# Who subtracts the low halves of the weights: VectorE call by call, or GpSimd in one stream

## The reference

```
h = rmsnorm(x, g);  proj = h @ w_in            # and so on, some 19 weight matrices
x = x + rmsnorm(f, g_post_ffn)                  # end of the first block
a, b = split(rmsnorm_2(x, norm_ffn) @ w_ffn_in) # feed-forward of the second block
x = x + (silu(a) * b) @ w_ffn_out
```

## Time and profile before

| | us |
|---|---|
| median of 3 runs | 1704.19 (1703.19 to 1706.45) |
| profiled execution, first to last instruction (span) | 1701.9 |
| TensorE matmul busy | 1630.8 (96%) |
| VectorE busy | 925.6 (54%) |
| ScalarE busy | 620.5 (36%) |
| GpSimd busy | 26.1 (2%) |

### The profile page before, as it was taken

One profiled execution on the slowest core, in us unless ns is written; L12 is line 12 of the kernel. 1 busy time (PEld: TensorE's weight loads), 2 busy tenths in 40 slices (PEclk: granted clock), 3 DMA queues, 4 the chain that ended last, 5 costly groups with the idle time before them and its releaser, 6 DMA issues.

```text
span 1701.9 us, 20773 instructions
## 1 busy us (share of the span) xinstructions
PE 1630.8 (96%) x7854; PEld 1342.2 (79%) x7854; DVE 925.6 (54%) x1471; ACT 620.5 (36%) x856; POOL 26.1 (2%) x17
## 2 busy tenths in 40 slices
PE   5999999999998999999999899899899999999999
PEld 5788666888876788888888668899668788888887
DVE  6343365644544777777334768888844444444322
ACT  6241333432233444444233355454334232222211
POOL 0000000000000000000001000110000000000000
PEclk9999999999998999999999999999558999999999
DMA  6402221222222122223323212022001222222332
GB/s 232 142 26 100 71 72 50 96 79 96 99 99 99 48 100 99 99 99 113 109 99 113 75 53 97 25 75 75 1 1 50 92 106 99 94 89 92 113 107 74
DMA packets 24890, 147.11 MB, mean 86 GB/s; under 512 B 2515, under 2 KB 5075, under 8 KB 8316
## 3 DMA queue, kind: packets, MB, share of 16 engines
q1 hardware_dynamic: 24828, 146.27, 24.7%
HBM read 144.13 MB, written 2.13 MB: 86 GB/s over the span
## 4 chain that ended last, share of the span: by engine, by line
PE 89%; DVE 5%; ACT 3%; issue 2%; DMA 0%; DVEq 0%; SPq 0%; ACTq 0%
PE bank L1537 26%; PE bank L1539 25%; PE bank L1538 25%; PE bank L1631 4%; PE bank L1649 3%; PE bank L1638 2%; PE bank L1881 1%; ACT w_hi L544 1%; PE bank L1851 1%; DVE w_lo L947 1%; PE bank L1660 1%; PE bank L1590 0%; DMA vec<-vec 0%; DVE diag L1001 0%; DVE h_lo L1016 0%
## 5 line engine op out<-in xcount | busy, mean ns | idle before, releaser
L947 DVE TENSOR_TENSOR w_lo<-raw,w_hi 128x2048 fp32r<-128x2048 f32 x123 | 281.8, 2291 | 400.6 <-ACT w_hi L544 400.3
L1537 PE MATMUL bank<-h_hi,w_hi 128*128 128x512 f32 (+1 forms) x1200 | 476.0, 397 | 11.1 <-DVE h_lo L1016 9.9
L1539 PE MATMUL bank<-h_hi,w_lo 128*128 128x512 f32 (+1 forms) x1200 | 470.1, 392 | 0.0
L1538 PE MATMUL bank<-h_lo,w_hi 128*128 128x512 f32 (+1 forms) x1200 | 469.7, 391 | 0.0
L544 ACT ACTIVATE w_hi<-raw 128x2048 fp32r<-128x2048 f32 x129 | 246.3, 1910 | 353.7 <-PE bank L1539 352.0
L1537 PEld LDWEIGHTS bank<-h_hi,w_hi 128*128 128x128 f32 (+1 forms) x1200 | 226.2, 188 | 65.1 <-DVE h_lo L1016 9.8
L1539 PEld LDWEIGHTS bank<-h_hi,w_lo 128*128 128x128 f32 (+1 forms) x1200 | 226.0, 188 | 49.1
L1538 PEld LDWEIGHTS bank<-h_lo,w_hi 128*128 128x128 f32 (+1 forms) x1200 | 226.3, 189 | 47.3 <-issue 1.0
L1537 PE MATMUL bank<-a_hi,w_hi 128*128 128x512 f32 x352 | 136.9, 389 | 0.0
L1538 PE MATMUL bank<-a_lo,w_hi 128*128 128x512 f32 x352 | 136.9, 389 | 0.0
L1539 PE MATMUL bank<-a_hi,w_lo 128*128 128x512 f32 x352 | 136.9, 389 | 0.0
(11 more groups left out here) (247 smaller groups left out, 2048.2 us busy)
## 6 DMA issues: line engine op xcount, KB each, us to landing
raw<-weights SPq DMA_DIRECT2D x129, 1024.0 KB, 4.8
toep<-bias_scratch SPq DMA_DIRECT2D x8, 448.0 KB, 4.6
x<-xT SPq DMA_DIRECT2D x1, 2048.0 KB, 14.7
outT<-x SPq DMA_DIRECT2D x8, 256.0 KB, 4.3
memT<-memT SPq DMA_DIRECT2D x1, 1024.0 KB, 5.9
mem2T<-mem2T SPq DMA_DIRECT2D x1, 1024.0 KB, 5.5
masks_in<-masks SPq DMA_DIRECT2D x1, 512.0 KB, 3.3
vec<-vec SPq DMA_DIRECT2D x1, 140.0 KB, 5.7
```

The costliest lines, as they stand in the source:

```text
L947: nc.vector.tensor_tensor(w_lo[m % 2][:, :], raw[m % 2][:, :], w_hi[m % 2][:, :].bitcast(F32), ALU.subtract).then_inc(lo_ready, 1)
L1537: nc.tensor.matmul(o, lh, rh, start=first, stop=False)
L1538: nc.tensor.matmul(o, lh, rl, start=False, stop=False)
L1539: return nc.tensor.matmul(o, ll, rh, start=False, stop=last)
```

## The change

VectorE's helpers `split_w` and `split_part` are gone, with all their calls. GpSimd gets a helper of the same name that makes the low halves of a range of slices, whole, one after the other, in the order of the loads. Before each it waits for its own one before (`lo_ready`) and for the rounding (`hi_ready`). Its earlier work stands between ranges: the masks and the fill of `sel` and `sfx`, which came right after the start, now follow the slices `mem_kv_2`, `idx` and the first of `hf`, and at every level from the second on one slice follows the suffix addition. The other engines' programs are as they were.

```diff
@@ gpsimd
             nc.gpsimd.memset(relb[NB:NB + 1, :], NEG).then_inc(set_up, 1)
+
+            def split_w(first, last):
+
+                for m in range(first, last):
+                    if m > first:
+                        pool.wait_ge(lo_ready, m)
+                    pool.wait_ge(hi_ready, m + 1)
+                    nc.gpsimd.tensor_tensor(w_lo[m % 2][:, :], raw[m % 2][:, :], w_hi[m % 2][:, :].bitcast(F32),
+                                            ALU.subtract).then_inc(lo_ready, 1)
+
+            pool.wait_ge(set_up, 2)
+            split_w(0, FIRST["iq"])
+            pool.wait_ge(lo_ready, FIRST["iq"])
             pool.wait_ge(mask_in, 32)
             nc.gpsimd.tensor_copy(masks[:, :, :], masks_in[:, :, :]).then_inc(set_up, 1)
             pool.wait_ge(set_up, 3)
+            split_w(FIRST["iq"], FIRST["idx"] + 1)
+            pool.wait_ge(lo_ready, FIRST["idx"] + 1)
             nc.gpsimd.memset(sel[:, :, :], 0.0).then_inc(set_up, 1)
             pool.wait_ge(set_up, 4)
+            split_w(FIRST["hf"], FIRST["hf"] + 1)
+            pool.wait_ge(lo_ready, FIRST["hf"] + 1)
             nc.gpsimd.memset(sfx[:, :], 0.0).then_inc(set_up, 1)
...
             nc.gpsimd.memset(aT[:, :, :], 0.0).then_inc(set_up, 1)
+            pool.wait_ge(set_up, 6)
+            split_w(FIRST["hf"] + 1, FIRST["sq"] + 2)
+            pool.wait_ge(lo_ready, FIRST["sq"] + 2)
...
                                         ALU.add).then_inc(suffix_ready, 1)
+                if lv:
+                    pool.wait_ge(suffix_ready, lv + 1)
+                    split_w(FIRST["sq"] + lv + 1, FIRST["sq"] + lv + 2)
+                    pool.wait_ge(lo_ready, FIRST["sq"] + lv + 2)
+            split_w(FIRST["sq"] + LEVELS + 1, NLOADS)
@@ vector
-            def split_w(m, i=None, per=0):
-
-                if i is None and m >= NLOADS:
-                    return
-                dve.wait_ge(hi_ready, m + 1 if i is None else m + 1 + per * i)
-                nc.vector.tensor_tensor(w_lo[m % 2][:, :], raw[m % 2][:, :], w_hi[m % 2][:, :].bitcast(F32),
-                                        ALU.subtract).then_inc(lo_ready, 1)
...
                 for m in range(loads):
-                    split_w(FIRST[name] + m + 1)
                     for t in (2 * m, 2 * m + 1):
...
             residual("mix", lambda j: mixed[:, j, :], "g_post_mix", "g_pre_ffn", range(KT))
-            split_w(FIRST["up"] + 2)
             norm_scale("ffn", S)
...
                 for m in range(2):
-                    if i is not None:
-                        split_w(FIRST["up"] + m + 4, i, 2)
-                    elif m:
-                        split_w(FIRST["up"] + 3)
                     for c in (2 * m, 2 * m + 1):
```

More of the change, by code:

```diff
@@ L1102, in _ @@
                 add_squares(j == 0, M, ssq_mem)
-                if j == 1:
-                    split_w(0)
-            split_w(1)
             dve.wait_ge(const_in, 32)
@@ L1109, in _ @@
                 add_squares(j == 0)
-                if j == 2:
-                    split_w(2)
                 if j == 5:
                     norm_scale("mem", M, keep=8)
-                    split_w(3)
                     dve.wait_ge(bank_free[6], turn(("spread", "mem")) + 1)
@@ L1119, in _ @@
                                                                     ALU.mult))
-            split_w(4)
-            split_w(5)
-            split_w(6)
             norm_scale("x", S, keep=0)
@@ L1127, in _ @@
                 normal("qm", t, qm[:, t, :])
-            split_w(FIRST["v"] + 1)
-            attention("mem", MHEADS * TT, None, lambda h, i: o_tok[:, i, h * MDH:(h + 1) * MDH],
-                      between=lambda s: s in (8, 9) and split_part(FIRST["q"], s - 8))
+            attention("mem", MHEADS * TT, None, lambda h, i: o_tok[:, i, h * MDH:(h + 1) * MDH])
             turned("turn_mem", 4, lambda j: br_hi[:, 8 + j, :], lambda j: br_lo[:, 8 + j, :])
@@ L1133, in _ @@
             times_rms("k", 2, lambda t: k[:, t, :])
-            split_w(FIRST["cc"] + 1)
             def toeplitz(h, i):
@@ L1141, in conv_branch @@
             def conv_branch(s):
-                for part_ in range(2):
-                    if s - part_ in CONV_STEPS:
-                        split_part(FIRST["cc"] + 2 + CONV_STEPS.index(s - part_), part_)
                 if s - 1 in CONV_TILE[4:8]:
@@ L1182, in _ @@
                     for m in range(3):
-                        split_w(FIRST["branch"] + 3 * half + m + 1, i, 6)
                         for t in range(2 * m, 2 * m + 2) if m < 2 else ():
@@ L1202, in _ @@
             for m in range(4):
-                split_w(FIRST["w_out"] + m + 1)
                 for j in (2 * m, 2 * m + 1):
@@ L1206, in _ @@
             norm_scale("mix", S)
-            split_w(FIRST["up"] + 1)
             wait_free(("w_out", KT - 1))
             residual("mix", lambda j: mixed[:, j, :], "g_post_mix", "g_pre_ffn", range(KT))
-            split_w(FIRST["up"] + 2)
             norm_scale("ffn", S)
@@ L1257, in _ @@
                 for m in range(3):
-                    if 3 * g + m + 2 <= 12:
-                        split_w(FIRST["down"] + 3 * g + m + 2)
                     if m:
@@ L1266, in _ @@
             norm_scale("down", S, extra=M)
-            split_w(FIRST["mem_kv_2"] + 1)
             dve.wait_ge(bank_free[3], turn(("down", 3), 1) + 1)
[L1270 to L1274, removed]
             out_tile = lambda j: down[:, j * S:(j + 1) * S]
-            residual("down", out_tile, "g_post_ffn", "norm_mix_2", range(4), between)
+            residual("down", out_tile, "g_post_ffn", "norm_mix_2", range(4))
             dve.wait_ge(w_used, FIRST["mem_kv_2"] + 2)
             residual("down", out_tile, "g_post_ffn", "norm_mix_2", range(4, KT))
-            split_w(FIRST["idx"])
             norm_scale("x_2", S, keep=0)
@@ L1309, in _ @@
                                          vec[:, VEC["sa_q_gain"]:VEC["sa_q_gain"] + 2], 64 ** -0.5, None, ALU.mult))
-            split_w(FIRST["hf"])
             dve.wait_ge(set_up, 4)
@@ L1340, in _ @@
             for m in range(2):
-                if m == 0:
-                    split_w(FIRST["hf"] + 1)
                 for t in (2 * m, 2 * m + 1):
@@ L1345, in _ @@
                     normal("hf", t, lf[:, t * S:(t + 1) * S])
-                split_w(FIRST["hf"] + m + 2)
                 top_keys(5 * m, 5 * m + 5)
@@ L1356, in _ @@
                     normal("hq", t, qf[:, t * S:(t + 1) * S])
-                split_w(FIRST["hq"] + m + 2)
                 top_keys(10 + 5 * m, 15 + 5 * m)
@@ L1383, in _ @@
                 if lv == LEVELS:
-                    split_w(FIRST["sq"] + lv + 1)
                     break
@@ L1402, in _ @@
                     head_norm(tok, tok_sq, S)
-                if lv:
-                    split_w(FIRST["sq"] + lv + 1)
                 top_keys((20, 24, 24, 24, 28, 28, 31)[lv], (24, 24, 24, 28, 28, 31, 34)[lv])
@@ L1466, in _ @@
             for m in range(4):
-                split_w(FIRST["w_out_2"] + m + 1)
                 for j in (2 * m, 2 * m + 1):
@@ L1474, in _ @@
                     add_squares(j == 0)
-            split_w(FIRST["up_2"] + 1)
-            split_w(FIRST["up_2"] + 2)
             norm_scale("ffn_2", S)
@@ L1482, in up_2_turn @@
                 it = 0 if i is None else i + 1
-                if i is not None:
-                    split_w(FIRST["up_2"] + 4, i, 2)
                 dve.wait_ge(prod, FT + 2 * it)
@@ L1488, in up_2_turn @@
                     normal(name, c, y[c][:, :])
[L1489 to L1492, removed]
                 dve.wait_ge(a_down, FT + 2 + 2 * it)
@@ L1510, in _ @@
             for g in range(4):
-                for m in range(3):
-                    split_w(FIRST["down_2"] + 3 * g + m + 2)
                 for j in (2 * g, 2 * g + 1):
```

## The result

| us | before | after |
|---|---|---|
| median of 4 runs each | 1704.84 (1703.19 to 1706.45) | 1744.86 (1743.46 to 1745.81) |
| ratio, 95% interval | | 1.0236 [1.0224, 1.0248] |
| span of the profiled execution | 1701.9 | 1743.3 |

The change makes the kernel 2.4% slower. Forecast were 1752 us within 1718 to 1788. On the span +47.5 was forecast and +41.4 came.

The account below looks back on a forecast made before the run. TensorE was taken to hold 89% of the path, VectorE 5%. Place terms of 42.5 us plus 5 for the clock, 47.5, on the 1701.9 span gave 1749.4; the median, 2.3 above the span, gave 1752 us (1718 to 1788).

Parts of the forecast that it names:

- Duration, 4.5 us: One GpSimd subtraction of 2048 elements takes 4.5 us (4.1 to 6.7), twice the corrected mean suffix addition.
- Start, +9: First four slices: 4.5 us locks delay VectorE's low halves and sums, and the scaling by 9.1 us; +9 us.
- Attention with convolution, +1, and memory attention, 0: Attention with convolution: VectorE relieved of six subtractions, then locked, +1 us (-1 to +4); no term for memory attention.
- `br_lo`, +4.5: GpSimd's subtraction takes the port pair amid eight two-input subtractions that TensorE consumes one by one; +4.5 us (0 to 4.5).
- Loop over `up`, 1.5 + 3: Subtraction stalls TensorE +1.5 us; turns of 22.0 us, 0.25 above TensorE, over 10 turns, plus 0.4 at entry: +3.
- Levels and last scaling, 1.1 + 4.2 + 3.3 + 2.1 = 10.7: Subtractions behind suffix additions lock VectorE: level 1 +1.1, level 2 +4.2, level 4 +3.3, last scaling +2.1 us.
- Norm of `ffn_2` and second slice of `up_2`, 1.5 + 2.2 = 3.7: Norm's products wait for GpSimd's subtraction, +1.5 us; at the second slice TensorE already waited for the subtraction, +2.2 us.
- Clock, +5: TensorE runs at a lower clock after new stands of 4 us or more; +5 us (0 to 12).
- half the locks: Rival: locks bite half as often, as waiting VectorE instructions may get in between subtractions; about 1731 us, chance 0.22.
- slow GpSimd: Rival: a GpSimd subtraction takes 5.5 us, the loop over `up` turns in 23.9 us; about 1788 us, chance 0.12.
- faster: Rival: GpSimd's subtraction holds nobody, what counts is 281.8 us off VectorE; about -4 us, 1700 us, chance 0.05.
- even: Rival: losses fall into unseen slack, so the time stays within 0.2%; chance 0.05.

Follow-up runs that it names:

- Experiment 1: Kernel before, with GpSimd making 11 of the 129 low halves (slices 8, 14 to 18, 80 to 84): 1700.09 us against 1704.38, ratio 0.9975.
- experiment 2: Kernel before, with GpSimd making 74 low halves (slices 8 to 36, 64 to 73, 80 to 84, 99 to 128): 1697.87 us, ratio 0.9959.
- experiment 7: Changed kernel, with the start's slices 0 to 7 subtracted by VectorE as before: 1736.03 us.
- experiment 8: Changed kernel, with slices 44 to 63, the loop over `up`, subtracted by VectorE again: 1739.45 us.
- experiment 4: Changed kernel, with the levels' seven slices 85 to 91 subtracted by VectorE as before: 1728.62 us.
- experiment 5: Changed kernel, all 129 low halves on GpSimd, which waits for VectorE's work at seven places (`br_lo` and levels): 1722.69 us.
- experiment 6: Changed kernel, with each GpSimd subtraction cut into four instructions of 512 elements, the signal on the last: 1735.14 us.

## Why the prediction was right, and where its terms were off

The rule was right as the prediction put it: the two engines exclude each other for a whole instruction, and the price is paid by VectorE operations of two SBUF inputs and SBUF scalar ones. The place-by-place sum is less good than its total, which came close by offsetting misses. In the trace after, the rows at level 2 that answer to the earlier trace rows show each link. The subtraction starts behind the suffix addition, 1.0 us before z ends (the prediction had it wait for z's end). It takes 5.48 us, because z still runs. `lf`, 1.23 us before, takes 5.29 and ends 1.08 us behind the subtraction:

```profile
1116.42 2.96 POOL L537 TENSOR_TENSOR sfx<-sfx,lf 128x1024 f32<-128x1024 f32 x1 [17.01 <-ACT ex L875]
1117.06 3.40 DVE L1358 TENSOR_TENSOR z<-qf,ex 128x1024 f32<-128x1024 f32 x1
1119.45 5.48 POOL L505 TENSOR_TENSOR w_lo<-raw,w_hi 128x2048 fp32r<-128x2048 f32 x1
1120.72 5.29 DVE L1364 TENSOR_TENSOR lf<-lf 128x1024 f32<-128x1024 f32 x1 [0.26 <-DVE z L1358]
...
1130.22 1.97 PE L1613 MATMUL bank<-ident,tok 128*128 128x128 f32 x8 [5.07 <-DVE tok L1267]
```

Step by step, on the span:

- *Duration, 4.5 us:* the rows are 4.50 at least and mostly 4.58 to 4.62, mean 4.64 with waits. The sum of seven suffix additions less three waits was good to 0.1. The Trainium skill's figure (GPSIMD Engine Reference, 3.1: 4497 ns) is the shortest row.
- *Start, +9:* +7.2. The replay held: the second rounding came 2.1 us late (2.2 forecast), the second subtraction ended 4.5 late (4.5), the third 6.8 late (6.4). The scaling behind the fourth subtraction came 8.3 us late (43.67 against 35.36), not 9.1, and TensorE's next wait, for `mk`, was 1.69 us in place of 2.59.
- *Attention with convolution, +1, and memory attention, 0:* -2.6 and -2.0. This is the largest miss, 5.6 us. I looked for what the lock adds, saw slack, and did not ask who waited for VectorE's subtraction there. The kernel before has TensorE waits of 1.35 us at 102.67 and 0.63 at 278.66 in just these stretches, behind `row` and its maximum, which read PSUM. Experiment 1 shows that this gain is real and can be had by itself. Of the 4.6 us gained, 2.4 are stands and 2.2 matmul time, mostly at a higher granted clock.
- *`br_lo`, +4.5:* +6.1. 0.7 of it is the last gate, which experiment 2 shows and which the prediction had at nothing. TensorE stands 3.57 us in the middle of the eight low parts (rows below) and then runs at the lower clock for a while; the stretch from rounding 37 to 38 cost 5.5, 3.9 and 3.9 us in three executions with the same order (the changed kernel and experiments 7 and 8). The stand is the term, the rest is the clock: between these roundings it was granted 0.90 in the changed kernel and 1.00 in the two others.

```profile
500.10 9.24 DVE L1014 TENSOR_TENSOR br_lo<-merged,br_hi 128x512 fp32r<-128x512 f32 x8
502.80 4.79 POOL L505 TENSOR_TENSOR w_lo<-raw,w_hi 128x2048 fp32r<-128x2048 f32 x1 [7.71 <-ACT w_hi L569]
508.19 0.50 PE L1490 MATMUL bank<-br_hi,w_hi 128*128 128x512 f32 x1 [3.57 <-DVE br_lo L1014]
```

- *Norms of `mix` and `ffn`, 1.4 and 1.5:* 1.1 and 1.65.
- *Loop over `up`, 1.5 + 3:* 4.3, of which 1.9 are the two stands at the entry and 2.4 the longer turns. The turn is 21.98 us where 22.0 was forecast, with twice a convolution step that starts inside GpSimd's subtraction and ends 0.54 us behind it. The rows answer to the earlier trace rows:

```profile
620.43 1.90 ACT L569 ACTIVATE w_hi<-raw 128x2048 fp32r<-128x2048 f32 x1
622.48 4.61 POOL L505 TENSOR_TENSOR w_lo<-raw,w_hi 128x2048 fp32r<-128x2048 f32 x1 [5.63 <-ACT w_hi L569]
623.18 4.45 DVE L1215 SCALAR_TENSOR_TENSOR y<-tap,vec,y 128x511 f32<-128x511 f32 x1 [2.00 <-ACT y L765]
...
634.22 4.61 POOL L505 TENSOR_TENSOR w_lo<-raw,w_hi 128x2048 fp32r<-128x2048 f32 x1 [7.13 <-ACT w_hi L569]
634.97 4.41 DVE L1215 SCALAR_TENSOR_TENSOR y<-tap,vec,y 128x511 f32<-128x511 f32 x1 [0.64 <-ACT y L765]
...
642.41 1.90 ACT L569 ACTIVATE w_hi<-raw 128x2048 fp32r<-128x2048 f32 x1
```

- *Residual, `x_2` and index scores, 2 + 3.2 + 2.2 = 7.4:* 6.1 together.
- *First level, -1.2:* -1.25. *Levels and last scaling, 1.1 + 4.2 + 3.3 + 2.1 = 10.7:* 12.7. Level 1 lost 2.0 (1.1), level 2 4.8 (4.2), level 4 and the last scaling 5.9 (5.4). Level 4 went as told: z lasts 4.96 us and TensorE waits 3.32 for `tok`.
- *Norm of `ffn_2` and second slice of `up_2`, 1.5 + 2.2 = 3.7:* 7.3. The stands are as forecast, 3.10 us against 0.76 and 2.04 against 0.38, together 4.0 more. But behind a stand of 3.10 us, which I had not counted among those that cost the clock, the same matmuls took longer in this execution. The window right there (length, busy us per engine, granted clock, DMA) has the granted clock at 0.86, a mixture of the lower level (1.2 GHz) and the full one (2.4 GHz), where it was 1.00:

```profile
1372.00:1384.00 12.00, 8.90 (x32) 6.85 (x31) 1.58 (x3) 2.15 (x2) 4.53 (x1) 0.86 0.27 98
1384.00:1394.00 10.00, 10.00 (x49) 8.40 (x48) 0.15 (x1) 2.22 (x2) 0.18 (x1) 1.00 0.01 2
```

The same window of the kernel before:

```profile
1338.00:1350.00 12.00, 11.24 (x50) 8.99 (x49) 3.76 (x4) 2.03 (x2) 0.00 (x0) 1.00 0.25 87
```

In experiments 4 and 5 the same stand of 3.10 us cost no clock. This is the window of experiment 4, with 40 matmuls in the 8.90 us in which the changed kernel made 32:

```profile
1358.52:1370.52 12.00, 8.90 (x40) 7.05 (x39) 1.58 (x3) 2.14 (x2) 4.52 (x1) 1.00 0.28 97
```

So the same two stands went with 3.3 us more matmul time in the changed kernel and with none in experiments 4 and 5. What decides it no run here shows.

- *Clock, +5:* +10.9 of busy time, within the bounds of 0 to 12, 8.5 of it outside the loop over `up`. Of the stands that the prediction named as 4 us or more, level 2 had 5.07, `br_lo` 3.57 and level 4 3.32, and in the start none exceeded 2.1. Cut by kind, the forecast missed twice: new stands of 42.5 us were forecast and 30.5 came (28.3 and the 2.2 us of the later first matmul), and 5 us of clock were forecast and 10.9 of matmul time came. The place terms of 42.5 and the measured losses by place (41.4) agree better only because the latter hold both kinds. The measured figures of the places above hold the matmul time already. Against them the 42.5 us of stands alone are 1.1 too high: 5.6 too much in the attentions, 1.8 in the start, 1.3 at `x_2` and 0.4 in small ones, against 1.6 too little at `br_lo`, 2.0 at the levels, 3.6 at `ffn_2` and 0.8 at the second attentions. That the forecast was as close as 0.4% is in part luck: gains not seen on one side, the clock on the other.
- *The rivals:* half the locks (1731), slow GpSimd (1788), faster and even are all refuted: every elementwise row of two SBUF inputs that started inside a subtraction ended behind it, and the duration is 4.6 us. "GpSimd holds nobody" was right for one class of rows only, those that read PSUM, and there it gave up to 4.6 us. The prediction also says that the rule speaks against the change at every slice. It doesn't: experiment 2 moved 74 slices at no cost but at the last gate.

## What to carry to other kernels

Work moved to GpSimd costs not its own time but the time of the VectorE operations that start while it runs, if they take both inputs, or a scalar operation's input, from SBUF; ask of each place which operation stands there and where its operands are. Beside VectorE operations that read PSUM it was free, and where VectorE's in-order stream delayed such reads it even gained: 11 of the 129 subtractions moved, chosen by place, gave -0.25%, 74 of them -0.4%, all of them +2.4%. Where all must move, hold GpSimd back behind VectorE's critical operation (22 us of the 40 came back), or cut its instruction so that the engines alternate (10 us). And judge a place by its stands: matmul time moved by several us between executions at places that no edit had touched.

## What the runs showed of the hardware

- The lock is given at instruction boundaries and alternates: no convolution step waited for more than one piece of GpSimd's in the loop of experiment 6 (the longest of 88 took 1.78 us), though the pieces stood back to back. A piece of 512 elements costs about 1.25 us (four in 5.0), the whole 4.6: each cut costs about 0.13.
- It works the other way, too: 5.48 us for a GpSimd subtraction that met z.
- Which rows were caught in the trace after: two SBUF inputs (all 21 convolution steps that started inside a subtraction), SBUF scalar operations on large tiles (`cy<-u,vec`: 3.74 us where it takes 0.48), an SBUF copy of 0.42 us that took 4.82. Not caught: everything from PSUM, fills, MAX8 and its replacement on SBUF, reciprocals, and the scalar operation on one column (`mx<-mx`, 12 of 12 at 0.15 us). A scalar operation on 4 columns (`st<-st`) took 1.64 us where it takes 0.17, but it met GpSimd's fill of `sel`, to whose end it lasted. None on 4 columns met a subtraction, so why the one on one column wasn't caught no run here shows.
- TensorE's clock behind a stand is not the same each time: behind the 3.57 us at `br_lo` it was granted 0.90 of full speed up to the next rounding in the changed kernel, 1.00 in experiments 7 and 8.
